# Two blocks on one core: the sums behind the last RMS norm before the second FFN go to GpSimd, and the first four FFN units are issued in another order

## The reference

```python
def rms_norm(x, g): ...            # x * rsqrt(mean(x*x) + 1e-6) * g

x = x + rms_norm(mixed @ w_out[l], norm_mix_post[l])
h = rms_norm(x, norm_ffn_pre[l])
f = (jax.nn.silu(h @ w_ffn_gate[l]) * (h @ w_ffn_up[l])) @ w_ffn_down[l]
x = x + rms_norm(f, norm_ffn_post[l])
```

## Time and profile before

| | |
|---|---|
| median of 3 runs | 2023.84 us |
| time of the profiled execution | 2025.35 us |
| its span in the trace | 2023.6 us |
| TensorE busy | 1963.2 us (97%) |
| VectorE, ScalarE, GpSimd busy | 1044.8, 634.5, 284.6 us |
| chain that ended last: TensorE's share | 87% |
| mean granted TensorE clock | 0.985 of full |

### The profile page before, as it was taken

The page is one execution under the profiler, slowest core; times in us unless marked ns, Lnnn a source line. Parts: engine busy times, 40 slices in busy tenths (PEclk is TensorE's granted clock), DMA queues, the critical chain, the costliest instruction groups (busy, mean ns, idle before and its releaser), DMA issues.

```text
span 2023.6 us, 23620 instructions
## 1 busy us (share of the span) xinstructions
PE 1963.2 (97%) x9642; PEld 1592.5 (79%) x9642; DVE 1044.8 (52%) x1456; ACT 634.5 (31%) x1053; POOL 284.6 (14%) x181
## 2 busy tenths in 40 slices
PE   6999999999999999999999999999999999999997
PEld 5788888888887888888888777877777878888885
DVE  6666633344455744344344765656676544344344
ACT  4333322233333432232234322224444333223221
POOL 3121220011111111010013000111111131011012
PEclk9999999999999999999999899999999989999998
DMA  4222223232311322322323111321121313323222
GB/s 160 72 69 79 76 92 107 93 94 73 88 58 48 120 94 94 104 94 96 96 89 97 63 63 63 104 73 63 53 63 37 120 53 104 96 96 100 94 87 70
DMA packets 52444, 171.87 MB, mean 85 GB/s; under 512 B 5879, under 2 KB 9279, under 8 KB 52336
## 3 DMA queue, kind: packets, MB, share of 16 engines
q1 hardware_dynamic: 51616, 169.21, 26.3%
q10 hardware_dynamic: 720, 1.15, 0.2%
HBM read 168.12 MB, written 2.21 MB: 84 GB/s over the span
## 4 chain that ended last, share of the span: by engine, by line
PE 87%; DVE 9%; ACT 3%; issue 1%; POOL 1%; DMA 0%; DVEq 0%; ACTq 0%; POOLq 0%
PE PS L1008 25%; PE PS L1010 25%; PE PS L1009 25%; PE PS L1112 1%; PE PS L1311 1%; PE PS L1127 1%; PE PS L1289 1%; DVE WL L1648 1%; PE PS L1333 1%; PE PS L1150 1%; PE PS L1073 1%; PE PS L1159 1%; PE PS L1173 1%; DVE AR L1676 1%; ACT WH L1376 1%
## 5 line engine op out<-in xcount | busy, mean ns | idle before, releaser
L1008 PE MATMUL PS<-HH,WH 128*128 128x512 f32 x1368 | 541.7, 396 | 14.1 <-DVE WL L1648 10.8
L1010 PE MATMUL PS<-HH,WL 128*128 128x512 f32 x1368 | 535.6, 392 | 0.0
L1009 PE MATMUL PS<-HL,WH 128*128 128x512 f32 x1368 | 535.2, 391 | 0.0
L1376 ACT ACTIVATE WH<-RAW 128x1024 fp32r<-128x1024 f32 (+2 forms) x320 | 326.0, 1019 | 405.7 <-PE PS L1010 405.6
L1648 DVE TENSOR_TENSOR WL<-RAW,WH 128x1024 fp32r<-128x1024 f32 (+2 forms) x257 | 318.7, 1240 | 234.6 <-ACT WH L1376 232.8
L1008 PE MATMUL PS<-AH,WH 128*128 128x512 f32 x1096 | 435.2, 397 | 2.3 <-DVE WL L1648 1.8
L1010 PE MATMUL PS<-AH,WL 128*128 128x512 f32 x1096 | 430.0, 392 | 0.0
L1009 PE MATMUL PS<-AL,WH 128*128 128x512 f32 x1096 | 429.8, 392 | 0.0
L1008 PEld LDWEIGHTS PS<-HH,WH 128*128 128x128 f32 x1368 | 258.7, 189 | 70.2 <-DVE WL L1648 10.8
L1010 PEld LDWEIGHTS PS<-HH,WL 128*128 128x128 f32 x1368 | 258.3, 189 | 54.7
L1009 PEld LDWEIGHTS PS<-HL,WH 128*128 128x128 f32 x1368 | 258.8, 189 | 52.1
(11 more groups left out here) (238 smaller groups left out, 1423.7 us busy)
## 6 DMA issues: line engine op xcount, KB each, us to landing
RAW<-wst SPq DMA_DIRECT2D x288, 512.0 KB, 3.4
RAW<-wst SPq DMA_DIRECT2D x16, 384.0 KB, 3.0
RAW<-wst SPq DMA_DIRECT2D x16, 256.0 KB, 2.5
XT<-xT SPq DMA_DIRECT2D x3, 512.0 KB, 7.8
AR<-scr SPq DMA_DIRECT2D x16, 64.0 KB, 4.1
AR<-scr SPq DMA_DIRECT2D x8, 128.0 KB, 4.7
AR<-w SPq DMA_DIRECT2D x2, 512.0 KB, 3.8
out<-XT SPq DMA_DIRECT2D x4, 256.0 KB, 2.0
```

Source lines behind the costliest of these rows:

```text
L1008: T.matmul(out, wh, XH[:, k, :], start=k == 0, stop=False)
L1009: T.matmul(out, wh, XL[:, k, :], start=False, stop=False)
L1010: m = T.matmul(out, wl, XH[:, k, :], start=False, stop=k == nk - 1)
L1376: t = A.activation(WH[:, i % NW, 0:n], RAW[:, i % NR, 0:n], ACT.Copy, scale=1.0)
```

## The change

`lead` no longer treats `n5`; a function of its own, `lead_slow`, issues four units: a, b and c take turns by two chunks; then half of d, one fold, a quarter of d, the spread, and the evictions around the last quarter of d. The partial folds are gone: GpSimd adds squares 1 to 6 into square 0 (`add_square`), behind its tile additions. In `post` the next tile's norm and addition are issued two tiles ahead of `post_next` and not one, `TMP` has four buffers, and VectorE adds tiles 0, 4 and 7 of `post2`.

```diff
+def lead_slow(e, a):
+
+    b, c, d = a + 1, a + 2, a + 3
+    for i in (a, b, c):
+        e.sum_bank("sum", i)
+    ahead(e, a)
+    for k in range(0, 8, 2):
+        for i in (a, b, c):
+            e.products(i, range(k, k + 2))
+    ahead(e, b)
+    ahead(e, c)
+    quarter(e, d, 0)
+    quarter(e, d, 1)
+    e.turn_bank("fold", "n5")
+    e.fold("n5")
+    quarter(e, d, 2)
+    e.turn_bank("spread", "n5")
+    e.spread("n5")
+    evict(e, a)
+    evict(e, b)
+    quarter(e, d, 3)
+    evict(e, c)
+    evict(e, d)
...
-    for j in range(9):
+    for j in range(10):
         if j < 8:
             e.post_norm(name, j)
-        if j:
-            e.post_next(name, j - 1)
-        if j < 8:
             e.post_add(name, j)
+        if j > 1:
+            e.post_next(name, j - 2)
+    if name == "post2":
+        for j in range(1, 7):
+            e.add_square(j)
...
-        ON_DVE = {"post2": (0,), "fpost2": (2, 5, 7)}
+        ON_DVE = {"post2": (0, 4, 7), "fpost2": (2, 5, 7)}
...
-            def fold_part(s, norm, part_):
-                b = s.bank["fold", norm]
-                if part_ == 0:
-                    s.free("fold", norm)
-                for j in (2 * part_, 2 * part_ + 1):
-                    pe.wait_ge(*at("sq", norm, j))
-                    for q in range(4):
-                        t = T.matmul(PS[:, b, q:q + 1], SN3[:, j, q * 128:(q + 1) * 128], con("mean", 0, 1),
-                                     start=j + q == 0, stop=j + q == 10)
-                if part_ == 3:
-                    t.then_inc(*pe_done["norm"].next("folded", norm))
...
                 dve.wait_ge(*at("factor", name))
-                if j > 1:
-                    dve.wait_ge(*at("x", name, j - 2))
-                t = V.scalar_tensor_tensor(out=TMP[name][j % 2], in0=SRC[name][:, j, :], scalar=col(name, j),
+                if j > 3:
+                    dve.wait_ge(*at("x", name, j - 4))
+                t = V.scalar_tensor_tensor(out=TMP[name][j % 4], in0=SRC[name][:, j, :], scalar=col(name, j),
...
+            def add_square(s, j):
+                s.add_up("n5", j)
```

More of the change, by code:

```diff
@@ L190 @@
     enter_attention = load_bias = attention_scores = attention_softmax = attention_turn = attention_out = none
-    choose_strips = unfold = shares = split_yb = enter_ffn = two_folds = two_spreads = fold_part = enter_gla = log_sigmoids = log_sigmoids_end = none
+    choose_strips = unfold = shares = split_yb = enter_ffn = two_folds = two_spreads = enter_gla = log_sigmoids = log_sigmoids_end = none
     decay = final_norm = gla_scores = gla_updates = gla_states = gla_outs = gla_scaled = gla_gated = none
@@ L195 @@
     few_scores = few_softmax = few_scale = few_turn = few_out = keep_yn = split_yn = none
-    post_factor = post_norm = post_next = post_add = finish = none
+    post_factor = post_norm = post_next = post_add = add_square = finish = none
 class Fill:
@@ L316, in lead @@
         return lead_two(e, a)
+    if norm == "n5":
+        return lead_slow(e, a)
     for q in range(4):
[L318 to L321, removed]
         if q == 0:
@@ L324, in lead @@
             e.sum_bank("sum", a)
-        if q == 3 and norm != "n5":
+        if q == 3:
             e.turn_bank("fold", norm)
@@ L535, in ffn @@
             lead(e, at, norm)
-            at, n = at + 3, n - 3
+            m = 4 if norm == "n5" else 3
+            at, n = at + m, n - m
         for i in range(at, at + n + 8):
@@ L859, in build @@
                 "fpost2": parts(4096, 512, 512, 512)}
-        TMP = {"post2": parts(nsa_at + 8192, 512, 512), "fpost2": parts(8704, 512, 512)}
+        TMP = {"post2": parts(nsa_at + 8192, *[512] * 4), "fpost2": parts(8704, *[512] * 4)}
         SRC = {"post2": NM3, "fpost2": OT2}
-        ON_DVE = {"post2": (0,), "fpost2": (2, 5, 7)}
+        ON_DVE = {"post2": (0, 4, 7), "fpost2": (2, 5, 7)}
         R1 = VT[:, :]
@@ L909, in sums @@
         def sums(name, n):
+            if name == "n5":
+                return SN3[:, n, :]
             a, b, acc = SUMS[name]
@@ L1662, in two_folds @@
                 t.then_inc(*dve_done["norm"].next("free", "fold", "n4"))
-            def fold_part(s, norm, part_):
-                if part_ == 3:
-                    s.fold(norm)
             def scaled(s, i, dst, p0=0, p1=128, scale=None, view=None):
@@ L2228, in post_add @@
                     dve.wait_ge(*at("post", name, j))
-                    V.tensor_tensor(XT[:, j, :], XT[:, j, :], TMP[name][j % 2], ALU.add).then_inc(
+                    V.tensor_tensor(XT[:, j, :], XT[:, j, :], TMP[name][j % 4], ALU.add).then_inc(
                         *dve_done["norm"].next("x", name, j))
@@ L2308, in post_add @@
                     pool.wait_ge(*at("post", name, j))
-                    G.tensor_tensor(XT[:, j, :], XT[:, j, :], TMP[name][j % 2], ALU.add).then_inc(
+                    G.tensor_tensor(XT[:, j, :], XT[:, j, :], TMP[name][j % 4], ALU.add).then_inc(
                         *pool_done["norm"].next("x", name, j))
```

## The result

| | before | changed |
|---|---|---|
| median of 9 runs | 2025.13 us | 2032.46 us |
| ratio, 95% interval | | 1.0038 [1.0028, 1.0048] |
| span of the profiled execution | 2023.6 us | 2029.5 us |
| first norm of `post2` to the first fold at the program's end | 374.0 us | 382.3 us |
| fold at the end to the first norm there | 5.2 us | 6.1 us |

A forecast was written before the change was run, and what follows sets the result against it. TensorE bounds the kernel (busy 97% of the span), so other engines count only where it stands still or runs slow. +7.3 us after `post2` and -1.5 at the end give +5.8: 2023.84 + 5.8 = 2029.6 us, range 2022.5 to 2033.0.

The forecast's parts named there:

- the edit that decides: Unit c among the first: TensorE waits at c's chunk 0 for low weights, ready at 1651.7, idle some 10 us.
- GpSimd keeps the port: Rival, chance 0.12: in `post2` GpSimd does all six sums first, c's low weights come at 1654.5; +2.8, 2032.4 us.
- The schedule through `post2`: Times from 1631.48 for additions, low parts (last at 1649.45) and c's split (1651.7), VectorE and GpSimd excluding each other.
- The turns of 1.70 us: Where both queue, VectorE instructions with two SBUF inputs and GpSimd ones take turns, 1.70 us a pair.
- From there to the fifth unit: From c's weights to the fifth unit: products 19.0, fold 1.70, spread 0.9, clock 1.9, eviction 0.3; sum 23.8 us.
- covered "barely": The split of d, costed at nothing: hidden by the last 12 products of b and c, 2.7 us; otherwise some tenths.
- the mark: Start of the fifth unit, after which the old order holds: forecast at 1675.5 against 1668.2.
- the same prices give the last addition at 2019.35: Program's end, `post` with four buffers: last addition at 2019.35 and not 2020.89, -1.5 us; bounds 0 and -2.8.
- the prediction's own signs of being wrong: c's low weights before 1649, no such idle time, or a last addition later than 1 us ahead of the old.
- the stretch: From `post2` into the second FFN: forecast to lose 7.3 us, read as the shift of the fifth unit's start.
- The sums slipping between VectorE's steps: Rival "Not slower", chance 0.22: sums hold up nothing in `post2`, c's low weights at 1648.7; 2026.6, or 2024.7 with clock kept.
- The intended gain: Rival "Faster", chance 0.10: c's weights no hindrance at the second FFN's start; -5.1 - 1.5, 2017.2 us.

The follow-up runs named there:

- the control: Kernel before with c's weights split ahead of the norms of `post2`: 2025.56 us (one run); first norm to fold at the end 373.95 against 374.03 us.
- c early: Changed kernel with c's weight split taken out of the lead and issued behind `post_factor`: 2018.62 us, 0.9980 of the kernel before.
- c early, new end: Changed kernel, c's split behind `post_factor`; at program's end eight buffers, VectorE does all norms, then adds tiles 4 to 7: 2016.87 and 2017.90 us, 0.9968 twice.

## Why the prediction was right

**The reading of the edit that decides was right.** It named the wait at c's first chunk, its length (some 10 us; 10.14) and its releaser. Putting c behind a and b, and putting c's split early, each took it away, and the loss with it; the control shows that the split by itself is no gain. The trace carries this, not the median: 2032.46 us also lies next to the 2032.4 of the rival in which GpSimd keeps the port, whose mechanism did not happen. And that the profiled execution took 2031.33 us with 2031.2 forecast is luck: its 3.2 us less ahead of the first norm hide that the rest was forecast too low.

**The schedule through `post2` was right to a few tenths.** Counted from the first norm, the low parts 0 to 4 were forecast at 4.0, 5.7, 8.1, 9.4 and 11.2 us and ended at 4.0, 5.7, 8.1, 9.4 and 11.1; the last at 18.0 and 17.8; c's weights at 20.2 and 20.0. The turns of 1.70 us, read from the program's start, carried it, and the run without sums gave the 3 us that were set for them.

**From there to the fifth unit:** 23.8 forecast, 24.6 measured (1648.21 to 1672.83). The fold, the spread and the loss of clock are as priced (nine products at 0.427, then 0.227). TensorE stood 0.3 us for the eviction of a, as said. What had not been counted is 0.15 us from the weights to the first product, the same again at d, whose split was covered "barely" and came some hundredths too late, and the slower first products behind the wait, the fold, the spread and the eviction. A further 0.4 us lies behind the mark (from the fifth unit to the first fold at the end 337.7 us against 337.3), where the forecast had nothing. The gap is the same in every kernel here with the new lead. Most of it is a wait for weights at the seventh unit, which the kernel before does not have there:

```profile
1682.69 1.22 DVE L1664 TENSOR_TENSOR WL<-RAW,WH 128x1024 fp32r<-128x1024 f32 x1 [0.33 <-ACT WH L1392]
...
1683.61 0.39 PE L1038 MATMUL PS<-HH,WL 128*128 128x512 f32 x1
...
1684.06 0.47 PE L1036 MATMUL PS<-HH,WH 128*128 128x512 f32 x1
```

The product comes 0.45 us behind the one before it instead of 0.23, and 0.15 behind the end of the split, the same 0.15 as at c; with the slower product behind it that makes 0.3 us. The rest is the restart behind the mark.

**The end was wrong.** The step that failed is "the same prices give the last addition at 2019.35": -1.5 us forecast, 0.0 measured. It is also one of the prediction's own signs of being wrong (a last addition later than 1 us ahead of the old one), and that sign came. The prices were right and the turn was not: where both engines became ready within some hundredths of a microsecond, I gave VectorE the port, and GpSimd got it; the norms then stood behind the addition. The forecast's other error has the same sign: the stretch cost 8.3 and not 7.3. So by the traces the forecast of 5.8 us was 2.5 too low, and it lies at the lower edge of the interval of the ratio. Without the end's 1.5 the sum would have been 2031.1; the measured ratio puts it at 2031.5 from the old median. Of the 2.9 us between the forecast 2029.6 and the measured 2032.46, 1.3 come from the median of the kernel before, which was 2023.84 in three runs and 2025.13 in nine.

**The rivals.** GpSimd keeping the port did not happen: turns were taken. The sums slipping between VectorE's steps did not happen. The intended gain exists, 4 us by the ratio of c early, but only with the edit that the change lacks.

## What to carry to other kernels

When an order is changed so that one more unit of work is interleaved, look up where each of its inputs is issued in every queue, the prefetch of its weights above all: an `ahead` two units deep is not deep enough for three units by turns. Work that is "free" on another engine has to be placed by the port it shares as well as by its due time, and a waiting instruction goes behind those that feed somebody else. A deeper buffer pays nothing while the engine behind it is bound by its own work.

## What the runs showed of the hardware

- Two instructions, one on VectorE with two SBUF inputs and one on GpSimd, excluded each other in every stretch read here; with both queues full they took turns at 1.70 us a pair (1.26 + 0.44). When GpSimd's next addition was already queued and VectorE's became ready within some hundredths of a microsecond, GpSimd's went ahead: recorded from 2018.74 against 2018.78, and the latter took 1.77 us instead of 0.7; the same at 2022.5.
- A split of 128x1024 that takes 1.22 us alone took 2.28 behind one GpSimd sum.
- TensorE came back from a 10 us wait at 1.2 GHz and stayed there for nine products, 3.97 us (1648.36 to 1652.33), at a cost of 1.9 us, what the price from the trace of before had been.
- One kernel's profiles differ by up to some 3 us ahead of the changed place and by 0.9 us at the end, where a spread runs at either clock. Distances inside a trace told apart what medians of ten runs could not, but they need the clock beside them: within one kernel (c early, new end) it rose 7.8 us behind the first norm in one profile and 10.1 in the other, with stretches of 369.6 and 370.1.
